# Even attention: weighted values per query block with tokens on partitions, row norm by accumulated squares

## The reference, cut to what matters

```python
s = jnp.einsum('bhqd,bkhd->bhqk', q_i, k).astype(jnp.float32) * scale
s = jnp.where(_block_mask(i, S), s, -jnp.inf)
p = jax.nn.softmax(s, axis=-1).reshape(B_, H, 2, Q_BLOCK, S)
w = p[:, :, 0] - lam * p[:, :, 1]
return jnp.einsum('bhqk,bkhe->bqhe', w.astype(v.dtype), v)
...
o = diff_attention(q, k, v, lam)
o = rms_norm(o, subln_w) * (1.0 - lambda_init)
return jnp.concatenate([u, o.reshape(B_, S, DIFF_V)], axis=-1)
```

## Time and profile before

| | |
|---|---|
| median of three runs | 1328.27 us |
| profiled execution | 1331.17 us |
| its span in the trace | 1329.4 us |
| TensorE busy | 1306.1 us (98%) |
| VectorE busy | 653.1 us (49%) |
| ScalarE busy | 498.2 us (37%) |
| SyncE's and ScalarE's DMA queues | 26% of the 16 DMA engines' span |

### The profile page before, as it was taken

The page is one execution under the profiler, slowest core; times in us unless marked ns, Lnnn a source line. Parts: engine busy times, 40 slices in busy tenths (PEclk is TensorE's granted clock), DMA queues, the critical chain, the costliest instruction groups (busy, mean ns, idle before and its releaser), DMA issues.

```text
span 1329.4 us, 17079 instructions
## 1 busy us (share of the span) xinstructions
PE 1306.1 (98%) x6413; PEld 1060.1 (80%) x6413; DVE 653.1 (49%) x936; ACT 498.2 (37%) x731; POOL 13.9 (1%) x22
## 2 busy tenths in 40 slices
PE   9999989999999999999999999999999999999997
PEld 6776547888888878888888988888888888878886
DVE  6676766644444442228656436434544444442224
ACT  6343325533333331125554444444433333332111
POOL 0000000000000000000001010000000000000000
PEclk9999989999999999999989999999999999999998
DMA  6232220332222233322212101001322222223221
GB/s 238 90 100 81 76 70 33 100 116 99 96 95 95 95 97 102 101 95 67 94 62 80 48 17 48 33 33 42 117 95 95 95 95 95 95 95 111 95 79 64
DMA packets 34080, 114.02 MB, mean 86 GB/s; under 512 B 4466, under 2 KB 4722, under 8 KB 34034
## 3 DMA queue, kind: packets, MB, share of 16 engines
q1 hardware_dynamic: 33266, 112.29, 25.5%
q10 hardware_dynamic: 768, 1.09, 0.3%
HBM read 106.90 MB, written 2.10 MB: 82 GB/s over the span
## 4 chain that ended last, share of the span: by engine, by line
PE 92%; DVE 3%; ACT 3%; DMA 1%; issue 1%; ACTq 0%; SPq 0%; DVEq 0%
PE PS L1372 90%; DMA raw<-w_stream 1%; PE PS L1448 1%; PE PS L1784 1%; DVE wring L951 1%; ACT wring L560 1%; DVE hbuf L1220 0%; DVE outT L1366 0%; DMA reps<-ub 0%; ACTq L676 0%; ACT HH L564 0%; PE PS L1665 0%; ACT lnsq L688 0%; DVE amax L1016 0%; DVE lnsq L1114 0%
## 5 line engine op out<-in xcount | busy, mean ns | idle before, releaser
L1372 PE MATMUL PS<-HH,wring 128*128 128x512 f32 x3096 | 730.8, 394 | 0.0
L1372 PEld LDWEIGHTS PS<-HH,wring 128*128 128x128 f32 x3096 | 577.5, 189 | 120.7 <-issue 3.4
L1372 PE MATMUL PS<-AA,wring 128*128 (+1 forms) x1320 | 303.0, 390 | 1.7 <-DVE ubuf L922 1.6
L1372 PEld LDWEIGHTS PS<-AA,wring 128*128 128x128 f32 x1320 | 247.3, 188 | 54.4 <-DVE ubuf L922 2.4
L922 DVE TENSOR_TENSOR ubuf<-PS,rstd 128x512 f32<-128x512 f32 x44 | 30.4, 691 | 198.1 <-PE PS L1372 198.1
L944 DVE TENSOR_TENSOR wring<-raw,wring 128x1024 fp32r<-128x1024 f32 x36 | 44.1, 1226 | 149.6 <-ACT wring L611 149.6
L931 DVE TENSOR_TENSOR wring<-raw,wring 128x1024 fp32r<-128x1024 f32 x88 | 107.5, 1222 | 0.9 <-ACT wring L603 0.4
L951 DVE TENSOR_TENSOR wring<-raw,wring 128x1024 fp32r<-128x1024 f32 x70 | 85.3, 1221 | 42.6 <-ACT wring L560 42.6
L560 ACT ACTIVATE wring<-raw 128x1024 fp32r<-128x1024 f32 x70 | 73.6, 1055 | 79.2 <-PE PS L1372 57.2
L598 ACT ACTIVATE AA<-ubuf 128x512 f32 x44 | 27.9, 633 | 198.4 <-DVE ubuf L929 198.4
L611 ACT ACTIVATE wring<-raw 128x1024 fp32r<-128x1024 f32 x36 | 38.2, 1061 | 155.5 <-PE PS L1372 155.5
(11 more groups left out here) (252 smaller groups left out, 1028.2 us busy)
## 6 DMA issues: line engine op xcount, KB each, us to landing
raw<-w_stream SPq DMA_DIRECT2D x194, 512.0 KB, 3.3
reps<-ub SPq DMA_DIRECT2D x48, 66.5 KB, 2.1
out_t<-outT SPq DMA_DIRECT2D x8, 256.0 KB, 2.2
xT<-x_t SPq DMA_DIRECT2D x3, 512.0 KB, 8.8
reps<-ub ACTq DMA_DIRECT2D x16, 66.5 KB, 2.2
first_raw<-w_stream SPq DMA_DIRECT2D x2, 512.0 KB, 9.8
rope<-rope_const SPq DMA_DIRECT2D x1, 576.0 KB, 6.8
consts<-shape_const SPq DMA_DIRECT2D x1, 576.0 KB, 7.7
```

What stands on the lines that cost most here:

```text
L1372: return nc.tensor.matmul(out, lhsT, rhs, start=start, stop=stop)
```

## The change

The weighted values are computed per unit, one slot after the unit's transposes: i+1 products with the transposed weights as the stationary operand and 128 columns of values moving. The result has tokens on partitions. ScalarE copies it (128x128) and squares it with an accumulating output, which gives the sum over the features as one column; so `sub_sum` and `sub_bc` go. `sub_ms` works on that column, `sub_mul` multiplies a head's four blocks by the reciprocal roots of their rows, and four transposes per head (`sub_t`) put the features on partitions again. The high part is then a scaled copy out of PSUM on ScalarE, and the low part a scaled difference on VectorE. WT shrinks to two units. The items of the last two slots, and those at the head of the output projection, stand in another order.

```diff
--- before.py
+++ after.py
@@ -121,6 +121,8 @@
             after[0].append(("gate", last[1]))
+        if 4 <= n < 17:
+            after[0].append(("diff_v", n - 4))
         if 3 <= n < 17:
@@ -130,15 +132,13 @@
             after[3].append(("diff_m", n - 1))
-        if n in (6, 10, 14):
-            after[2].append(("diff_v", (n - 6) // 4))
         if n == 16:
-            after[3] += [("sub_sum", 0), ("sub_ms", 0), ("sub_root", 0), ("sub_rec", 0)]
+            after[3] += [("sub_ms", 0), ("sub_root", 0), ("sub_rec", 0)]
         if n == 17:
-            after[0] += [("diff_t", 14), ("diff_w", 15), ("sub_bc", 0)]
-            after[1] += [("sub_mul", 0), ("sub_bc", 1), ("sub_hi", 0)]
-            after[2] += [("diff_t", 15), ("sub_mul", 1), ("sub_lo", 0), ("sub_hi", 1), ("sub_bc", 2)]
-            after[3] += [("diff_v", 3), ("sub_mul", 2), ("sub_hi", 2), ("sub_lo", 1)]
+            after[0] += [("diff_v", 13), ("diff_t", 14), ("diff_w", 15), ("sub_mul", 0)]
+            after[1] += [("sub_t", 0), ("diff_v", 14), ("sub_mul", 1), ("sub_hi", 0)]
+            after[2] += [("diff_t", 15), ("sub_t", 1), ("sub_lo", 0), ("sub_mul", 2), ("sub_hi", 1)]
+            after[3] += [("sub_t", 2), ("diff_v", 15), ("sub_lo", 1), ("sub_hi", 2)]
         taps = [("tap", (c, k)) for c in range(4) for k in range(DIRECT) if TAP_SLOTS[c][k] == n]
@@ -161,9 +161,8 @@
     order += [("sub_lo", 2), ("ln_sum", 0)] + [("ln_centre", c) for c in range(4)]
-    order += [("out_heads", (0, 0, 2)), ("sub_sum", 1), ("out_heads", (0, 2, 3)), ("sub_ms", 1), ("sub_root", 1), ("sub_rec", 1),
-              ("ln_sq_add", 1), ("ln_sq_add", 2), ("out_heads", (1, 0, 3)), ("ln_sq_add", 3), ("sub_bc", 3), ("sub_mul", 3), ("sub_hi", 3),
-              ("sub_lo", 3), ("ln_var_sum", 0), ("out_heads", (2, 0, 3)), ("ln_var", 0), ("ln_root", 0), ("ln_rec", 0), ("ln_bc", 0),
+    order += [("out_heads", (0, 0, 3)), ("sub_ms", 1), ("sub_root", 1), ("sub_rec", 1), ("ln_sq_add", 1), ("sub_mul", 3), ("ln_sq_add", 2),
+              ("out_heads", (1, 0, 3)), ("sub_t", 3), ("sub_hi", 3), ("sub_lo", 3), ("ln_sq_add", 3), ("ln_var_sum", 0), ("out_heads", (2, 0, 3)), ("ln_var", 0), ("ln_root", 0), ("ln_rec", 0), ("ln_bc", 0),
               ("out_heads", (3, 0, 3))]
@@ -312,7 +311,8 @@
     first_raw, _ = at("first_raw", [FIRST - RAW, TILE], f32, q)
-    WT, q = at("WT", [2, NB, S], f32, q)
+    WT, q = at("WT", [2, NB, P], f32, q)
+    osq, q = at("osq", [P], f32, q)
     assert q <= TOP, (q, TOP)
@@ -327,7 +327,7 @@
     assert q <= at_H + 32768
-    oT, osq = qk[:, 0:H], qk[:, H:2 * H]
+    oT = qk[:, 0:H]
 
@@ -439,7 +439,7 @@
     DIFF_T, DIFF_V = 0, 1
-    SUB_BANK, SUB_STAT = (5, 4, 5, 7), (4, 6)
+    SUB_BANK = (5, 4, 5, 7)
     LN_MEAN, LN_VAR, LN_BC = 4, 5, 4
@@ -638,15 +638,14 @@
 
-        def wt_copy(u, sem_t, sem_c, dst, bank, sem_pv):
-
-            h, i = UNITS[u]
-            act.wait_ge(sem(sem_t), u + 1)
-            if h >= 2 and i == 0:
-                act.wait_ge(sem(sem_pv), h - 1)
-            nc.scalar.activation(dst[:, h % 2, 0:i + 1, blk(i)],
-                                 PS[:, bank, 0:(i + 1) * P].rearrange("p (j c) -> p j c", c=P),
-                                 ACT.Copy).then_inc(sem(sem_c), 1)
+        def weights_copy(u):
+
+            i = u % NB
+            act.wait_ge(sem("diff_t"), u + 1)
+            if u >= 2:
+                act.wait_ge(sem("diff_pv"), u - 1)
+            nc.scalar.activation(WT[:, u % 2, 0:i + 1], PS[:, DIFF_T, 0:(i + 1) * P].rearrange("p (j c) -> p j c", c=P),
+                                 ACT.Copy).then_inc(sem("diff_wt"), 1)
 
@@ -677,11 +676,13 @@
             elif kind == "diff_t":
-                wt_copy(a, "diff_t", "diff_wt", WT, DIFF_T, "diff_pv")
+                weights_copy(a)
             elif kind == "diff_v":
                 act.wait_ge(sem("diff_pv"), a + 1)
-                nc.scalar.activation(oT[:, a], PS[:, DIFF_V], ACT.Copy)
-                nc.scalar.activation(osq[:, a], PS[:, DIFF_V], ACT.Square).then_inc(sem("diff_osq"), 1)
+                h, i = UNITS[a]
+                nc.scalar.activation(oT[:, h, blk(i)], PS[:, DIFF_V, blk(a % 2)], ACT.Copy)
+                nc.scalar.activation(osq[:], PS[:, DIFF_V, blk(a % 2)], ACT.Square,
+                                     accum_out=ost[:, 0, a:a + 1]).then_inc(sem("diff_osq"), 1)
             elif kind == "ln_centre":
@@ -701,8 +702,8 @@
             elif kind == "sub_hi":
-                act.wait_ge(sem("y_scaled"), a + 1)
-                nc.scalar.activation(AA[:, a, 0], oT[:, a], ACT.Copy).then_inc(sem("y_hi"), 1)
+                act.wait_ge(sem("y_turned"), a + 1)
+                nc.scalar.activation(AA[:, a, 0], PS[:, SUB_BANK[a]], ACT.Copy, scale=subw[:]).then_inc(sem("y_hi"), 1)
 
@@ -1128,8 +1129,8 @@
                 g = slice(*SUB_COLS[a])
-                dve.wait_ge(sem("stat_mm"), a + 1)
-                V.tensor_scalar(ost[:, 0, g], PS[:, SUB_STAT[a], g], 1.0 / P, 1e-6, ALU.mult, ALU.add).then_inc(sem("stat_ms"), 1)
+                dve.wait_ge(sem("diff_osq"), SUB_COLS[a][1])
+                V.tensor_scalar(ost[:, 0, g], ost[:, 0, g], 1.0 / P, 1e-6, ALU.mult, ALU.add).then_inc(sem("stat_ms"), 1)
                 if a == 0:
@@ -1137,10 +1138,13 @@
             elif kind == "sub_mul":
-                dve.wait_ge(sem("stat_bc"), a + 1)
-                V.scalar_tensor_tensor(oT[:, a], oT[:, a], subw[:], PS[:, SUB_BANK[a]], ALU.mult, ALU.mult).then_inc(sem("y_scaled"), 1)
+                dve.wait_ge(sem("stat_rec"), 1 + a // 3)
+                rows_ = oT[:, a].rearrange("p (b c) -> p b c", c=P)
+                V.tensor_tensor(rows_, rows_, per_head(ost[:, 1, NB * a:NB * (a + 1)]), ALU.mult).then_inc(sem("y_scaled"), 1)
             elif kind == "sub_lo":
-                y_lo(a + 1, a, oT[:, a])
+                dve.wait_ge(sem("y_hi"), a + 1)
+                V.scalar_tensor_tensor(AA[:, a, 1], PS[:, SUB_BANK[a]], subw[:], AA[:, a, 0].bitcast(f32),
+                                       ALU.mult, ALU.subtract).then_inc(y_ready, 1)
         out_proj(1, T_OUT0, E_OUT0)
@@ -1448,9 +1452,11 @@
 
-        def weighted_values(h, wt, v, bank):
-            for j in range(NB):
-                last = mm(PS[:, bank, j * P:S], v[:, j, blk(h)], wt[:, h % 2, j, j * P:S], j == 0, j == NB - 1)
+        def weighted_values(u):
+
+            h, i = UNITS[u]
+            for j in range(i + 1):
+                last = mm(PS[:, DIFF_V, blk(u % 2)], WT[:, u % 2, j], vtk[:, j, blk(h)], j == 0, j == i)
             return last
@@ -1540,17 +1546,17 @@
             elif kind == "diff_v":
-                pe.wait_ge(sem("diff_wt"), NB * (a + 1))
-                if a:
-                    pe.wait_ge(sem("diff_osq"), a)
-                weighted_values(a, WT, vtk, DIFF_V).then_inc(sem("diff_pv"), 1)
+                pe.wait_ge(sem("diff_wt"), a + 1)
+                if a >= 2:
+                    pe.wait_ge(sem("diff_osq"), a - 1)
+                weighted_values(a).then_inc(sem("diff_pv"), 1)
             elif kind == "ln_sum":
                 pe.wait_ge(sem("ln_added"), 3)
-                pe.wait_ge(sem("y_scaled"), 2)
+                pe.wait_ge(y_ready, 2)
                 mm(PS[:, LN_MEAN], ones, ln_total[:]).then_inc(sem("ln_mean_mm"), 1)
...
                 pe.wait_ge(sem("ln_sq_added"), 3)
-                pe.wait_ge(sem("y_scaled"), 3)
+                pe.wait_ge(y_ready, 3)
                 for b in range(NB):
@@ -1559,21 +1565,14 @@
                 last.then_inc(sem("ln_rstd_bc"), 1)
-            elif kind == "sub_sum":
-                heads_ = range(3) if a == 0 else (3,)
-                pe.wait_ge(sem("diff_osq"), heads_[-1] + 1)
-                pe.wait_ge(sem("diff_exp"), 30 + 2 * a)
-                for h in heads_:
-                    for b in range(NB):
-                        last = token_sum(PS[:, SUB_STAT[a], 4 * h + b:4 * h + b + 1], osq[:, h, blk(b)])
-                last.then_inc(sem("stat_mm"), 1)
-            elif kind == "sub_bc":
-                pe.wait_ge(sem("stat_rec"), 1 + a // 3)
+            elif kind == "sub_t":
+                pe.wait_ge(sem("y_scaled"), a + 1)
+                pe.wait_ge(sem("diff_exp"), 30 if a < 3 else 32)
                 if a == 2:
-                    pe.wait_ge(sem("y_scaled"), 1)
+                    pe.wait_ge(y_ready, 1)
                 for b in range(NB):
-                    last = spread(PS[:, SUB_BANK[a], blk(b)], ost[:, 1, 4 * a + b:4 * a + b + 1])
-                last.then_inc(sem("stat_bc"), 1)
+                    last = nc.tensor.transpose(PS[:, SUB_BANK[a], blk(b)], oT[:, a, blk(b)], ident)
+                last.then_inc(sem("y_turned"), 1)
             elif kind == "out_heads":
@@ -1581,7 +1580,7 @@
                     elif n == 1:
-                        pe.wait_ge(sem("diff_osq"), H)
+                        pe.wait_ge(sem("diff_osq"), H * NB)
                 for k in range(k0, k1):
```

## The result

The changed kernel took 1330.49 us (median of 20 runs, 1327.28 to 1332.89); the kernel before, run beside it on the same chip, 1326.68 us (20 runs, 1321.86 to 1329.85). The ratio is 1.0031, 95% interval 1.0024 to 1.0039: the change costs about 4 us, where 1.8 us of gain was forecast. The median lies just inside the stated range of 1320.5 to 1330.5 us, but on the other side of the kernel before. The profiled execution of the changed kernel took 1332.07 us, 0.90 us more than the one of before. Two differences are thus to be explained: 0.9 us between two profiled executions, and 4 us between medians. One is read from the trace, the other needed the experiments.

The account below looks back on a forecast made before the run. TensorE, busy 98% of the span, was taken as the bound, except where VectorE's chain holds it near the end. Terms -0.8 + 0 + 0.2 - 1.2 = -1.8 us gave a median of 1326.5 us, 8-in-10 range 1320.5 to 1330.5.

Parts of the forecast that it names:

- stretch 4: 179.03 to 204.71 us, plus-times counted from 179.03: VectorE's chain holds TensorE, so only -1.2 us, between -1.6 and -0.8.
- Behind 204.71: Output products after the variance's product: same products as before, no waits before them, 0 us.
- the 4 us before the first transposes: Near 183 us: TensorE reaches the transposes at about +4.4 and waits 4 us for VectorE's row scaling, done at +8.4.
- The rival with that mechanism: End of the edit: new standstills at half clock cost output products 3.4 us, +2.0 in all, 1330.3 us; chance 0.18.
- Stretch 1: To 160.14 us, end of slot 14: TensorE's own time, -6.39 + 4.84 + 1.7 - 0.81 - 0.14 = -0.8 us.
- 0.22n - 0.08: Slots to 160.14 us: cost in us of a small group of n matmuls; 11 groups, 26 matmuls, 4.84 us.
- The wait at 136 us: TensorE's 0.8 us wait before the rope product would go, because unit 7 fills it: -0.81 us.
- the second: TensorE's other query-key wait, 0.6 us before a rope product: hides unit 8, 0.14 us; VectorE stays the bound.
- The cut: Slots 5, 6, 9, 10, 11, 14: splitting twelve projection matmuls into two sixes costs 0.28 us each, 1.7 in all.
- Stretch 2: 160.14 to 170.36 us: fixed by the replica DMAs, 0 us; unit 11 goes into the 3.40 us wait, leaving about 2.4.
- Stretch 3: 170.36 to 179.03 us, the last scores: unit 12, one matmul, +0.2 us; clock assumed to fall as before.
- TensorE's own saving of 8 us: 179.03 to 204.71 us: on TensorE alone -9.0 + 1.4 - 0.4 = -8.0 us, mostly lost to VectorE's chain.

Follow-up runs that it names:

- fill_both: Changed kernel plus unread 512-column float32 products, three before the first transposes and two before the variance's product: 1325.51 us, 0.9999 of the kernel before.
- fill_first: Changed kernel plus three unread 512-column float32 products before the first transposes only: 1326.50 us, 1.0000 of the kernel before.
- fill_second: Changed kernel plus two unread 512-column float32 products before the variance's product only: 1325.79 us, 0.9996 of the kernel before.
- early_scaling: Changed kernel with head 0's row scaling moved right behind the reciprocal roots: 1326.33 us, 1.0003 of the kernel before.
- before_again: The kernel before, unchanged, run as if new and profiled a second time: 1327.53 us, 1.0004 of the kernel before.
- the three groups: Runs of the kernel before beside each group of experiments: 35, 35 and 33 runs, medians 1325.82, 1327.08 and 1325.74 us.
- first group: 35 runs of the unchanged kernel before: median 1325.82 us, 1326.65 at clock 0.992; the changed kernel's first 20 runs: 1327.16 at 0.992.
- third: 33 runs of the unchanged kernel before: 1326.52 us at clock 0.992; the changed kernel, run again beside them: 1326.41 at 0.992.
- tail_later: Changed kernel with the last head's scaling, transposes, high and low part behind the three sums of squares: 1325.70 us, 0.9996 of the kernel before.
- before_fill_replica: Kernel before plus three unread 512-column float32 products in its wait for the replica DMAs: 1325.24 us, 0.9987 of the kernel before.
- three_fixes: Changed kernel with early head 0 scaling, the mean in its own bank, and the last head's work behind the sums: 1325.00 us, 0.9986 of before.

## Why the prediction was wrong

**The step that failed** is the end of stretch 4: "Behind 204.71 the products are the same, with no waits before them: 0." The same products took 2.95 us more, because the 2.2 us wait before the variance's product is followed by half clock. The wait itself had been forecast ("2 to 3 us before the variance's product"), and so had the 4 us before the first transposes (3.5 measured). What was missing from the sum was their price in clock, of which it took 0.4 us for the first and nothing for the second. The forecast added up instructions and waits; a wait of TensorE can cost its own length and what runs at half speed behind it. fill_both, fill_first, fill_second and early_scaling show the mechanism: in the changed kernel it is worth some 4 us of the median. The single term of 2.95 us is surer in kind than in size, since before_again lost 1.35 us in the same place behind a wait of 1.0 us.

The rival with that mechanism and "2 x 1.7 = 3.4 us" had 0.18 of the chance. That its 1330.3 us all but meet the measured 1330.49 is luck: it forecast +2.0 us on a median of three runs that was 1.6 us too high, and the change was +3.8. The chance was too small because the trace of before had shown the mechanism already, with 1.7 us lost behind a standstill of 3.4 us, and the forecast itself put two more standstills into the kernel.

**The base.** The profiled execution of before was taken as its typical one, 2.9 us over the median of three runs and 4.5 over that of twenty. Its mean clock was 0.989, that of the 103 runs in the three groups 0.9922 to 0.9928. So before had clock to lose, which one execution at a low clock did not show. The changed kernel runs at 0.9890, and 26 of its 30 runs lie between 0.988 and 0.990. The difference of 0.0035 times 1.08 us per 0.001 is 3.8 us, which with +0.5 (first group) or -0.1 us (third) at equal clock is the measured slowdown to within half a us. In the two profiles only some 1.7 us of it (0.03 x 55) are seen between 160 and 215 us. Against the profile of before_again there is as much again from 660 to 700 us (0.91 against 0.96), in code that the change leaves alone; whether that is chance is not shown.

**Stretch 1: right in kind, short in size.** Small groups stand 0.14, 0.37, 0.58 and 0.81 us before what follows (73.62 to 73.76, 127.12 to 127.93), as 0.22n - 0.08 says. The wait at 136 us is gone, and 0.4 of the second is left. The cut was mis-sized. From starts and not from busy times, a run of six takes 1.47 us (127.93 to 129.40), one of twelve 2.85 (78.09 to 80.94) and one of eighteen 4.20 (before, 78.53 to 82.73); twelve and six are 4.32. A cut costs 0.12 us, not 0.28: busy times of neighbours overlap, and I had added them. Six cuts are 1.0 us less than forecast, and the stretch gave -1.74 us instead of -0.8.

**Stretch 2: right.** The replica wait is 1.9 instead of 2.4 us: unit 11's group and its cut took 1.2 us there instead of 1.0, and the replicas came 0.26 us sooner behind the slot's end. **Stretch 3:** +0.6 instead of +0.2; the first convolution of 16 records was busy 3.40 us, mostly at half clock, and unit 12's group right behind it moved the next start by 0.59 us instead of 0.2.

**Stretch 4: right in its first half.** First transposes at +8.25 (forecast +8.4), at half clock 1.11 us instead of 0.66. The mean's product came at +16.95, not +15.85: behind the half-speed group of unit 14 ScalarE's copies came later, VectorE waited 1.7 us for them, and the first low part began at +11.8 (188.77) instead of +10.8. That VectorE's chain holds TensorE, and that TensorE's own saving of 8 us isn't to be had there, came as forecast. tail_later shows that part of what was left lies in the order: 1.0 to 1.8 us at equal clock. early_scaling points the same way with 0.7 +-0.4 us, which is hardly clear of noise.

**Transposes and the clock.** The clock fell in the stretch with the first transposes, which would fit the Trainium skill, "TensorE: Matmul & The Clock Gate", section on PE-mode transpose, by which transposes don't count as activity as matmuls do. fill_first speaks against transposes as the cause here: three groups of four between 183.61 and 188.09 us (the last row holds two), they and their neighbours at full clock, once the standstill before them was down to 0.7 us. Whether transposes count like matmuls no run here shows, since they stand between real products.

```profile
183.61 0.66 PE L1582 MATMUL PS<-consts,qk 128*128 128x128 f32 x4 [0.72 <-DVE qk L1143]
184.10 0.83 PE L1376 MATMUL PS<-vtk,WT 128*128 128x128 f32 x6
184.87 1.92 PE L1376 MATMUL PS<-reps,cw 128*32 128x512 f32 x16
...
187.21 1.04 PE L1582 MATMUL PS<-consts,qk 128*128 128x128 f32 x8
```

## What to carry to other kernels

Where TensorE is nearly always busy, price a new wait twice: its length, and what may run behind it at half clock. Taking matmuls out of a stretch in which another engine's chain holds TensorE turns work into standstill, and can make the kernel slower, as here. Split a change that has a part on the busy engine and a part on a chain: here per-unit groups alone gain 0.31%, and with the other half the whole loses 0.31%. And compare the mean clock of the profiled execution with that of the timed runs before taking differences from it.

## What the hardware showed

- A run of this kernel is 1.08 us longer for 0.001 less mean granted clock, and one kernel's runs range from 0.989 to 0.997 (before, 103 runs). By that slope it is 8.6 us, twice the effect of the change.
- In the 55 us from 160 to 215 us the clock took only the values 0.88, 0.91, 0.94, 0.97 and 1.00 in fourteen profiled executions: half clock comes in portions that cost some 1.7 us each (0.03 x 55 = 1.65, or 1.70 to 1.72 read in slices of 2 us).
- Filling a standstill with useless products made the kernel shorter, by 0.3% of the whole for five products of 512 columns.
- Half clock followed waits of 1.9 and 2.2 us as well as of 3.5 us. It sometimes came at once (transposes 1.11 us) and sometimes with the second group behind the wait (fill_second: transposes 0.65 us, then a small group of 1.36 instead of 0.83 and a convolution of 3.02 instead of 1.92 us). Waits of 1.8 to 2.0 us for the replicas had none behind them in fill_both, fill_first, tail_later and three_fixes. Which waits it follows in a given execution stays open.
- Half clock also followed 24 single-column records without a standstill of over 0.8 us ahead of them (before_fill_replica: 0.50 from 180 to 185 us, TensorE busy throughout).
